# Gated recurrence and retention with 128x128 states between chunks, and v turned on its own signal

## The reference

```python
def hgrn2_chunk_scan(q, k, v, g):   # per head; g = log of the forget gate
    def step(state, inp):
        b = cumsum(gc)
        att = einsum('tk,sk,tsk->ts', qc, kc, exp(b_t - b_s) where t >= s)
        o = att @ vc + (qc * exp(b)) @ state
        state = exp(b_last)[:, None] * state + (kc * exp(b_last - b)).T @ vc
        return state, o
# run forwards, and backwards on the reversed sequence; the two outputs are summed

def retention(q, k, v):             # per head, decay exp(log_g) a position, chunks C = 128
    scores = (q @ k.T) * exp((i - j) * log_g) for i >= j, inside a chunk
    kv_n = (k * exp((C - 1 - j) * log_g)).T @ v
    state = state * exp(C * log_g) + kv_n
    o = scores @ v + (q * exp((i + 1) * log_g)) @ state_before_the_chunk
```

## Time and profile before

| | |
|---|---|
| median of 3 runs | 3102.72 us (3102.54 to 3104.55) |
| the profiled execution's own time | 3104.33 us |
| its span, first to last instruction | 3102.5 us |
| mean granted clock of TensorE | 0.993 |
| PE / DVE / ACT / POOL busy | 98% / 53% / 40% / 42% |

### The profile page before, as it was taken

How to read it: one execution, slowest core, us unless ns; L and a number is a source line. 1 busy time by engine, 2 the same in 40 slices (tenths; PEclk the granted TensorE clock), 3 DMA queues, 4 the chain that set the end, 5 groups by cost and what they waited for, 6 DMA issues and landing times.

```text
span 3102.5 us, 44873 instructions
## 1 busy us (share of the span) xinstructions
PE 3026.5 (98%) x15566; PEld 2400.8 (77%) x15566; DVE 1641.6 (53%) x2261; ACT 1235.7 (40%) x2180; POOL 1312.5 (42%) x1006
## 2 busy tenths in 40 slices
PE   8999999999999999998999999999999999999997
PEld 6877778777777787786877777788777777777886
DVE  5367666554454514657565664462175656645412
ACT  5545444333334433344333333453343333334532
POOL 4443434333334244453434444344534444444444
PEclk9999999999999999999999999999999999999999
DMA  6222212222122223223322222224333222222422
GB/s 236 105 80 107 81 68 81 70 80 81 68 79 84 109 95 136 95 99 128 119 85 89 85 82 82 82 94 149 110 132 106 85 89 85 82 82 82 147 97 95
DMA packets 60872, 305.60 MB, mean 99 GB/s; under 512 B 5712, under 2 KB 6096, under 8 KB 29776
## 3 DMA queue, kind: packets, MB, share of 16 engines
q1 hardware_dynamic: 38224, 259.54, 23.4%
q10 hardware_dynamic: 22528, 44.50, 4.1%
HBM read 285.67 MB, written 18.35 MB: 98 GB/s over the span
## 4 chain that ended last, share of the span: by engine, by line
PE 48%; issue 27%; POOL 14%; DVE 7%; DVEq 2%; ACT 1%; POOLq 1%; DMA 0%; ACTq 0%; SPq 0%
PE z L313 38%; POOL w_low L250 13%; DVE work L1440 2%; DVEq L1522 1%; DVE work L1429 1%; PE turned L313 1%; PE z L329 1%; PE scores L313 1%; PE scores L510 1%; PE o_bank L517 1%; PE scores L539 1%; PE o_bank L549 1%; PE scores L529 1%; PE v_bank L346 1%; PE z L346 1%
## 5 line engine op out<-in xcount | busy, mean ns | idle before, releaser
L250 POOL TENSOR_TENSOR w_low<-w_raw,w_high 128x512 fp32r<-128x512 f32 x932 | 1251.8, 1348 | 1770.1 <-ACT w_high L692 1763.1
L313 PE MATMUL z<-u_high,w_high 128*128 128x512 f32 x3408 | 1368.4, 402 | 2.9 <-POOL w_low L250 2.2
L313 PE MATMUL z<-u_high,w_low 128*128 128x512 f32 x3408 | 1329.0, 390 | 0.0
L313 PE MATMUL z<-u_low,w_high 128*128 128x512 f32 x3408 | 1328.2, 390 | 0.0
L692 ACT ACTIVATE w_high<-w_raw 128x512 fp32r<-128x512 f32 x928 | 577.6, 628 | 1274.4 <-PE z L313 1174.6
L313 PEld LDWEIGHTS z<-u_high,w_high 128*128 128x128 f32 x3408 | 640.1, 188 | 156.8 <-issue 24.0
L313 PEld LDWEIGHTS z<-u_low,w_high 128*128 128x128 f32 x3408 | 640.4, 188 | 140.9 <-issue 11.5
L313 PEld LDWEIGHTS z<-u_high,w_low 128*128 128x128 f32 x3408 | 639.7, 188 | 136.0
L1591 DVE TENSOR_TENSOR work<-work 128x512 f32<-128x512 f32 x87 | 99.9, 1148 | 364.5 <-ACT work L939 350.6
L1253 DVE TENSOR_TENSOR work<-z,work 128x512 f32<-128x512 f32 x110 | 76.1, 692 | 166.4 <-PE z L313 145.4
L1281 DVE SCALAR_TENSOR_TENSOR work<-z,work 128x512 f32<-128x512 f32 x56 | 38.7, 692 | 189.1 <-PE z L313 188.5
(11 more groups left out here) (261 smaller groups left out, 3077.5 us busy)
## 6 DMA issues: line engine op xcount, KB each, us to landing
w_raw<-in_wt SPq DMA_DIRECT2D x241, 1024.0 KB, 4.8
out_hT<-work ACTq DMA_DIRECT2D x8, 1024.0 KB, 8.0
work<-out_hT ACTq DMA_DIRECT2D x8, 1024.0 KB, 10.4
work<-in_xT SPq DMA_DIRECT2D x4, 1024.0 KB, 18.4
e_scratch<-work ACTq DMA_DIRECT2D x1, 4096.0 KB, 16.8
work<-in_xT ACTq DMA_DIRECT2D x4, 1024.0 KB, 10.5
work<-in_dec ACTq DMA_DIRECT2D x12, 256.0 KB, 2.6
work<-rope_tables ACTq DMA_DIRECT2D x10, 256.0 KB, 2.9
```

The costliest lines, as they stand in the source:

```text
L250: pool.tensor_tensor(WL[:, 4 * q:4 * q + 4, :], RAW[:, t.odd, 512 * q:512 * q + 512].rearrange("p (k c) -> p k c", k=4), WH[:, 4 * q:4 * q ...
L313: mm = pe.matmul(bank[:], w[:, k, :], u[:, k, :], start=(k == 0 and n == 0), stop=(k == KT - 1 and n == 2))
```

## The change

Recurrence: levels 8 and 9 go. At point 9 PE turns three chunks of keys for each direction (into TP[0] and TP[1]), ACT copies them; at point 10 PE multiplies each turned chunk with v, which gives six 128x128 state shares, and DVE chains them (state times the chunk's total gate, plus the next share). At point 12, not 13, PE makes the output chunk by chunk: the weights inside the chunk times v, plus the forward and the backward state times the queries, 10 matmuls of 128 columns. AT is one row. The next head's preparation waits for that output. Products of level 8 go; `qk_ready` counts 4 a head and `lv_done` 3.

Retention: inside chunks of 128 only, with states between them. v is turned at point 0 when its projected tile has been freed. At point 1 PE turns three chunks of keys and makes four score blocks of 128 columns; ACT copies the turned keys, scaled by the decay. State shares are made at point 3, chained by DVE with a constant. At point 6 PE makes the output in 7 matmuls of 128 columns. `take_retention` (point 13) multiplies q by its decay where q was copied. The decay table keeps its size; its first 257 columns are used.

```diff
-        RA = [0, S, 2 * S - P, 3 * S - 3 * P]
+        RA, RST, RKT = 0, 1, 2
+        D_MASK, D_QUERY, D_KEY = 0, P, 2 * P
+        KFT, KBT = 12, 13
...
@@ PE, hg_work
                 if p == 9:
-                    pe.wait_ge(sem("qk_ready"), j * 5 + 4)
-                    pe.wait_ge(sem("cmp_free"), PRIMED + j * 2 + 1)
-                    for c in range(4):
...
-                        mm = pe.matmul(SC[0][:, c * P:(c + 1) * P], kk, qq, start=True, stop=True)
-                    mm.then_inc(sem("lv_done"), 1)
-                if p == 11:
-                    pe.wait_ge(sem("qk_ready"), j * 5 + 5)
+                    pe.wait_ge(sem("qk_ready"), j * 4 + 4)
                     pe.wait_ge(sem("hvn_ready"), j + 1)
                     pe.wait_ge(sem("hro_ready"), PRIMED + j)
-                    for c in range(4):
-                        bank = TP[c // 2]
...
-                        mm = pe.matmul(bank[:, (c % 2) * 256:(c % 2) * 256 + 256], kk, qq, start=True, stop=True)
-                    mm.then_inc(sem("lv_done"), 1)
-                if p == 13:
+                    for c in range(3):
+                        t, u = slice(c * P, (c + 1) * P), slice((c + 1) * P, (c + 2) * P)
+                        pe.transpose(TP[0][:, t], row(KF)[:, t], IDN[:])
+                        mm = pe.transpose(TP[1][:, t], row(KB)[:, u], IDN[:])
+                    mm.then_inc(sem("hk_turned"), 1)
+                if p == 10:
+                    pe.wait_ge(sem("hk_ready"), j + 1)
+                    pe.wait_ge(sem("cmp_free"), PRIMED + j * 2 + 2)
+                    for c, (bank, at) in enumerate(((SC[0], 0), (SC[0], 2 * P), (SC[1], 0))):
+                        d = 3 - c
+                        pe.matmul(bank[:, at:at + P], row(KFT)[:, c * P:(c + 1) * P], row(HVN)[:, c * P:(c + 1) * P],
+                                  start=True, stop=True)
+                        mm = pe.matmul(bank[:, at + P:at + 2 * P], row(KBT)[:, (d - 1) * P:d * P], row(HVN)[:, d * P:(d + 1) * P],
+                                       start=True, stop=True)
+                    mm.then_inc(sem("hkv_done"), 1)
+                if p == 12:
                     pe.wait_ge(sem("at_ready"), j + 1)
-                    pe.wait_ge(sem("x9_free"), j + 1)
+                    pe.wait_ge(sem("hst_ready"), j + 1)
                     pe.wait_ge(sem("hg_done"), PRIMED + j)
                     for c in range(4):
-                        mm = pe.matmul(OB[:], row(HVN)[:, c * P:(c + 1) * P], row(AT + c), start=(c == 0), stop=(c == 3))
+                        t = slice(c * P, (c + 1) * P)
+                        pe.matmul(OB[:, t], row(HVN)[:, t], row(AT)[:, t], start=True, stop=False)
+                        if c:
+                            mm = pe.matmul(OB[:, t], view(0, SF[c], [[1, P]]), row(QF)[:, t], start=False, stop=(c == 3))
+                        if c < 3:
+                            mm = pe.matmul(OB[:, t], view(0, SBW[c], [[1, P]]), row(QB)[:, t], start=False, stop=True)
                     mm.then_inc(sem("hav_done"), 1)
@@ PE, ret_work
                 if p == 0:
-                    turn_v(row(VTA), (sem("rqt_ready"), j + 1), "rv_turned")
-                if 1 <= p <= 4:
-                    c = p - 1
-                    pe.wait_ge(sem("ra_ready"), PRIMED + j * 4 + max(c - 1, 0))
-                    pe.matmul(SC[c % 2][:, 0:S - c * P], row(KTR)[:, c * P:(c + 1) * P], row(QT)[:, c * P:S],
-                              start=True, stop=True).then_inc(sem("rs_done"), 1)
+                    l, h = divmod(j, RET_HEADS)
+                    turn_v(row(VTA), (sem("z_free"), T_L2 + l * PER_LAYER + R_RET + 4 * h + 3 - T_HGG), "rv_turned")
+                if p == 1:
+                    pe.wait_ge(sem("rqt_ready"), j + 1)
+                    if j:
+                        pe.wait_ge(sem("rro_ready"), j)
+                    for c in range(3):
+                        mm = pe.transpose(TP[1][:, c * P:(c + 1) * P], row(KTR)[:, c * P:(c + 1) * P], IDN[:])
+                    mm.then_inc(sem("rk_turned"), 1)
+                    pe.wait_ge(sem("ra_ready"), PRIMED + j)
+                    for c in range(4):
+                        t = slice(c * P, (c + 1) * P)
+                        mm = pe.matmul(SC[0][:, t], row(KTR)[:, t], row(QT)[:, t], start=True, stop=True)
+                    mm.then_inc(sem("rs_done"), 1)
+                if p == 3:
+                    pe.wait_ge(sem("rvn_ready"), j + 1)
+                    pe.wait_ge(sem("rkt_ready"), j + 1)
+                    for c in range(3):
+                        t = slice(c * P, (c + 1) * P)
+                        mm = pe.matmul(SC[1][:, t], row(RKT)[:, t], row(VN)[:, t], start=True, stop=True)
+                    mm.then_inc(sem("kv_done"), 1)
                 if p == 6:
...
+                    pe.wait_ge(sem("state_ready"), j + 1)
                     pe.wait_ge(sem("ret_done"), PRIMED + j)
                     for c in range(4):
-                        mm = pe.matmul(OB[:, c * P:S], row(VN)[:, c * P:(c + 1) * P], view(0, RA[c], [[1, S - c * P]]),
-                                       start=(c == 0), stop=(c == 3), skip_group_check=True)
+                        t = slice(c * P, (c + 1) * P)
+                        mm = pe.matmul(OB[:, t], row(VN)[:, t], row(RA)[:, t], start=True, stop=(c == 0))
+                        if c:
+                            mm = pe.matmul(OB[:, t], row(RST)[:, (c - 1) * P:c * P], row(QT)[:, t], start=False, stop=True)
@@ ACT
                 if p == 9:
-                    act.wait_ge(sem("lv_done"), j * 5 + 4)
...
+                    act.wait_ge(sem("hk_turned"), j + 1)
+                    copy(row(KFT)[:, 0:3 * P], TP[0][:, 0:3 * P])
+                    copy(row(KBT)[:, 0:3 * P], TP[1][:, 0:3 * P], "hk_ready")
+                if p == 12:
                     act.wait_ge(sem("hav_done"), PRIMED + j + 1)
...
+                if p == 1:
+                    act.wait_ge(sem("rk_turned"), j + 1)
+                    copy(row(RKT)[:, 0:3 * P], TP[1][:, 0:3 * P], "rkt_ready", scale=row(DEC)[:, D_KEY:D_KEY + 1])
                 if p == 5 and load is not None:
-                    act.wait_ge(sem("ra_ready"), PRIMED + j * 4 + 4)
+                    act.wait_ge(sem("ra_ready"), PRIMED + j + 1)
+                    act.wait_ge(sem("rkt_ready"), j + 1)
                     act.dma_start(row(DEC), dec[load]).then_inc(sem("dec_loaded"), 16)
@@ DVE
+            def take_retention(n):
+                v.drain()
+                v.wait_ge(sem("dec_loaded"), n * 16 + 16)
+                v.tensor_tensor(row(QT).rearrange("p (c t) -> p c t", c=4), row(QN).rearrange("p (c t) -> p c t", c=4),
+                                view(DEC, D_QUERY, [[0, 4], [1, P]]), ALU.mult)
+                v.tensor_copy(row(KTR), row(KN)).then_inc(sem("rqt_ready"), 1)
...
@@ hg_prepare
-                    v.wait_ge(sem("lv_done"), j * 5 + 5)
+                    v.wait_ge(sem("hav_done"), PRIMED + j + 1)
@@ hg_work
                 if p == 9:
-                    products(j, 8)
                     v.wait_ge(sem("dia_free"), PRIMED + j + 1)
...
+                if p == 10:
+                    v.wait_ge(sem("hkv_done"), j + 1)
+                    v.tensor_copy(view(0, SF[1], [[S, 2], [1, P]]), SC[0][:, 0:2 * P].rearrange("p (a t) -> p a t", a=2))
+                    for c, bank, at in ((1, SC[0], 2 * P), (2, SC[1], 0)):
+                        v.drain()
+                        d = 3 - c
+                        v.scalar_tensor_tensor(out=view(0, SF[c + 1], [[1, P]]), in0=view(0, SF[c], [[1, P]]),
+                                               scalar=view(TT + 1, TOTAL + c, [[1, 1]]), in1=bank[:, at:at + P],
+                                               op0=ALU.mult, op1=ALU.add)
...
+                    i.then_inc(sem("hst_ready"), 1)
@@ ret_work
-                if 1 <= p <= 4:
...
+                if p == 1:
+                    v.wait_ge(sem("rs_done"), j + 1)
+                    v.tensor_tensor(row(RA).rearrange("p (c t) -> p c t", c=4), SC[0][:].rearrange("p (c t) -> p c t", c=4),
+                                    view(DEC, D_MASK, [[0, 4], [1, P]]), ALU.mult).then_inc(sem("ra_ready"), 1)
+                if p == 3:
+                    v.wait_ge(sem("kv_done"), j + 1)
+                    i = v.tensor_copy(row(RST)[:, 0:P], SC[1][:, 0:P])
+                    for c in (1, 2):
+                        v.drain()
+                        i = v.scalar_tensor_tensor(out=row(RST)[:, c * P:(c + 1) * P], in0=row(RST)[:, (c - 1) * P:c * P],
+                                                   scalar=CHUNK_DECAY[j % RET_HEADS], in1=SC[1][:, c * P:(c + 1) * P],
+                                                   op0=ALU.mult, op1=ALU.add)
+                    i.then_inc(sem("state_ready"), 1)
...
@@ constants
-        dec[h] = np.where(dd >= 0, np.exp(np.maximum(dd, 0) * np.log1p(-2.0 ** (-5.0 - h))), 0.0)
+        g, n = np.log1p(-2.0 ** (-5.0 - h)), a + 1.0
```

(32 more changed lines are left out.)

36 lines of the change are left out of this document (8 added, 28 removed).

## The result

The changed kernel takes 3073.2 us (median of 4 runs, 3071.6 to 3074.0), the kernel before, beside it on the same chip, 3102.6 (4 runs, 3102.5 to 3104.6): ratio 0.9903, 95% interval 0.9886 to 0.9920. That is 29.5 us less; 28.0 were forecast.

What follows compares the result with a forecast made beforehand. The prediction took PE's instruction stream as the bound. Savings of 14.5 (recurrence), 10.2 (retention) and 3.3 us (early turn of v) sum to 28.0, giving a forecast of 3075 us, range 3069 to 3087.

Steps and rivals of the forecast that it cites:

- The bound: PE, busy 98% of the span, bounds the kernel; a microsecond taken from its stream is worth nearly a microsecond.
- Recurrence, forecast 14.5: Eight recurrence heads: 6.06 us of PE stream removed, 4.25 added; 1.81 saved a head, 14.5 us in all.
- Retention, forecast 10.2: Twelve retention heads: scores and values, 2.16 us each, removed, 3.47 added; 0.85 saved a head, 10.2 us in all.
- The turn, forecast 3.3: Retention's turn of v at point 0, on its own signal, loses a 0.33 us wait in ten heads: 3.3 us.
- the price of nothing for the product: Retention: DVE's q product takes 0.69 us where a copy took 0.43; the extra 0.26 hides in 0.50 idle.
- Point 1 to 3, margin 0.5: Retention: ACT's new key copy ends 0.5 us before PE's state matmuls need it, the narrowest margin; no cost.
- States of the recurrence, 2.2 us against 5.5: Recurrence, point 10 to 12: DVE makes the states in some 2.2 us, PE wants them 5.5 later; no cost.
- Rival 1: Retention's states come late if the q product takes 1.79 us; PE waits, total 3079 to 3085 us; chance 0.08.
- Rival 2: Retention's period is set by DVE's chain and stays at 51.96 us; 13.5 not gained, total 3088; chance 0.07.
- Rival 3: Weight loads bound PE's narrow matmuls, from a pitch of 0.153 us up; 25.5 us slower, total 3128; chance 0.02.
- Better case: PE's waits for ACT's copies at point 1 of three recurrence heads go: some 5 us more, total 3070; chance 0.07.

Runs made afterwards that it cites:

- e3: Kernel before with only retention's turn of v on its own signal, the scores at point 1 waiting for q and k; 3098.8 us, ratio 0.9986.
- e8: Changed kernel with retention's four score blocks and DVE's mask product at point 2 instead of point 1; 3074.0 us, ratio 0.9909.
- e4: Changed kernel with retention's turn of v back behind the signal of the q and k copies; 3080.2 us, ratio 0.9924.
- e5: Changed kernel with one extra 384-column copy on ACT ahead of retention's key copy; 3075.2 us, ratio 0.9909.
- e6: Changed kernel with three extra 384-column copies on ACT ahead of retention's key copy; 3085.8 us, ratio 0.9947.
- e2: Kernel before with only the retention part and early turn of v, recurrence as before; 3086.0 us, ratio 0.9945.
- e7: Changed kernel with the recurrence's six state matmuls made twice into the same banks; 3083.3 us, ratio 0.9934.
- e9: Changed kernel with ACT's sines one point earlier in the first recurrence steps and dilated attention's turn of v on its own signal; 3069.6 us, ratio 0.9892.
- e1: Kernel before with only the recurrence part of the change, retention as before; 3087.1 us, ratio 0.9948.

## Why the prediction was right, point by point

- **The bound.** PE's stream sets the time: 30.3 us less of PE's busy time, 30.5 less span. All sums of PE's work came out in the span at full price.
- **Recurrence, forecast 14.5.** Measured 14.8; the period is 53.01 to 53.11 in the even steps, forecast about 53.0. Four of the eight steps, the fourth to the seventh, give 1.78 to 1.84, forecast 1.81; the surplus comes from the first two and the last (1.98, 1.96, 1.92). The waits for states at point 12 that were allowed nothing are not there.
- **Retention, forecast 10.2.** Measured from e3 to after: 619.98 - 608.16 = 11.8. The steady step gives 51.57 - 50.63 = 0.94, not 0.85. The term that was mis-sized is found by pricing each block of small matmuls in the traces of e3 and after, from its start to the second projection matmul behind it, less one pitch of 0.227 (us a head, mean of three steps in each layer):

  | | forecast | measured |
  |---|---|---|
  | removed: four score blocks | 2.16 | 0.866 + 0.653 + 0.440 + 0.225 = 2.18 |
  | removed: the values | 2.16 | 2.16 |
  | added: points 1, 3 and 6 | 3.47 | 1.226 + 0.679 + 1.565 = 3.47 |
  | the rest of the stream behind the removed blocks, beyond its pitch | nothing | 0.18 |
  | the same behind the added blocks | nothing | 0.11 |

  The added records cost what the forecast said. The score blocks were priced 0.02 low by the values block. The other 0.07 was put at nothing: behind a block some of the projection matmuls start 0.229 to 0.237 after each other, not 0.227, and the five old blocks left 0.18 us of this, the three new ones 0.11. No run shows why some blocks leave 0.04 and others 0.01; their number is not it (e8). The rest of the 11.8, 0.5 us, lies in layer 1's step into differential attention, which in e3 waited longer.
- **The turn, forecast 3.3.** Alone 3.3 (e3), as ten times 0.37 less what the next unconverted turn takes back. Inside the change it is 6.8 (e4), because the product of q would have made the wait longer. The forecast had both terms, 0.33 of wait and 0.26 of product, but summed them as if independent: the price of nothing for the product holds only with the early turn.
- **Point 1 to 3, margin 0.5.** 0.56 in ten heads (e5, e6), some 5 us in the first head of each layer. It is the place where the next addition to ACT would be paid.
- **States of the recurrence, 2.2 us against 5.5.** DVE takes 1.8, with 3.5 to spare until the output at 428.66:

```profile
423.41 0.42 DVE L1413 COPY work<-scores 128x256 f32<-128x256 f32 x1 [2.00 <-PE scores L445]
...
424.85 0.34 DVE L1420 SCALAR_TENSOR_TENSOR work<-work,scores 128x128 f32<-128x128 f32 x1
426.14 0.69 DVE L1282 TENSOR_TENSOR work<-z,work 128x512 f32<-128x512 f32 x1 [0.95 <-PE z L320]
```

- **Rival 1** asked for a product of q at 1.79. All twelve, by the source view of that line (ns min/median/max):

```profile
L1330 DVE TENSOR_TENSOR work<-work x12: 691/693/827, 1500.1 to 2597.0; 128x512 f32<-128x512 f32 x12
```

  At most 0.83, so its condition was not met. The traces also show when such a product gets slow. Ten of the twelve meet no POOL instruction and take 0.69. The two of 0.83, the first of each layer, begin while a subtraction of POOL is running, and end 0.55 us after it:

```profile
1498.85 1.55 POOL L257 TENSOR_TENSOR w_low<-w_raw,w_high 128x512 fp32r<-128x512 f32 x1 [0.98 <-ACT w_high L721]
```

```profile
1500.12 0.82 DVE L1330 TENSOR_TENSOR work<-work 128x512 f32<-128x512 f32 x1
```

  The level products of the kernel before show the same. The 13 that took 1.77 to 1.79 all began while POOL was subtracting and ended 0.55 after it; the other 51, during some of which POOL began, took 0.68 to 0.69. The Trainium skill, page SBUF — State Buffer, section Who interferes with whom, ties such a slowdown to GpSimd reading SBUF at the same time; these traces agree. So this rival hung on POOL being idle when the product begins, as the prediction said.
- **Rival 2** is refuted by the period of 50.63, and by e2 and e3, where two edits on PE each shorten it: DVE's chain follows.
- **Rival 3** is refuted by e7. The Trainium skill, page Perfetto Trace Analysis, section Identifying the Most-Contended Engine, names two measures for PE, its useful floating-point work and the busy share of its weight loads, and the prediction took up the second. Here that share rose from 77% to 78% while the kernel became 1% faster; by itself it would have spoken against the change, and the pitch decided.
- **Better case.** The waits at point 1 stayed, as forecast, since their cause, the sines, moves with PE. e9 shows both that they hang on the sines and that they were worth 3.0 us.

The gain is 1.5 us larger than forecast; the retention steps give 1.1 of it (12 x 0.94 less 10.2), and the rest is within what two executions differ by.

## What to carry to other kernels

Where one engine is busy throughout, price an edit by the pitch from start to start of that engine's records and not by their shown durations; count both what goes and what comes in the same unit, and the sum holds to a few per cent. Then look at what the added work waits for on its slowest neighbour, and measure the margin there by putting spare work ahead of it. When a wait is cured by giving an instruction its own signal, look at the next one of the same kind: it inherits the wait, and is often cured by the same line.

## What the runs showed that was not expected

- A 128-column full-precision matmul with its own weight load costs PE 0.223 us of stream (e7), although its two loads are shown with 0.19 each.
- A block of small matmuls also stretches the projection matmuls behind it, by 0.01 to 0.04 us in all. It is small, but it was most of what the forecast of the retention step lacked.
- A DVE product of two SBUF operands that begins while POOL is subtracting ends 0.55 us after POOL does; one that has begun before POOL keeps its 0.69.
- Splitting such work into one more block between projection matmuls costs 0.014 us (e8), although the first projection matmul behind a block is shown 0.1 longer (0.48 against 0.39).
- An idle time of PE understates what a wait costs, since it is counted from the modelled end of the record ahead: shown as 0.17 us it gave 0.37 a step when it went (e1 to e3), shown as 0.44 it cost 0.63 (e4). The gap from start to start, less the pitch, comes closer: 0.33 and 1613.40 - 1612.58 - 0.23 = 0.59. Most of what is still missing is in the transposes themselves: from their start to the second projection matmul behind them PE takes 0.73 us after such a wait and 0.67 without one (e3).
